# Weight blocks 160 instead of 128 columns apart in the panels that multiply x, and a separate buffer for the norms' sums

## What is computed

```
for l in range(2):
    hn = rmsnorm(x, g_mix_pre[l])
    m  = mixer_even(hn) if l == 0 else mixer_odd(hn)     # hn @ w_in (1024 x 2048, or 1024 x 3072),
                                                         # gating or recurrence or short convolution,
                                                         # then @ w_out (1024 x 1024)
    x  = x + rmsnorm(m, g_mix_post[l])
    hn = rmsnorm(x, g_ffn_pre[l])
    f  = square(relu(hn @ mlp_up[l])) @ mlp_down[l]      # 1024 x 4096 and 4096 x 1024
    x  = x + rmsnorm(f, g_ffn_post[l])
```

## Time and profile before

| | |
|---|---|
| median of 3 runs | 2115.69 us |
| the profiled execution | 2116.21 us |
| its span in the trace | 2114.1 us |
| TensorE busy (matmuls) | 2105.2 us, 100% of the span |
| VectorE (DVE) busy | 1187.2 us, 56% |
| ScalarE (ACT) busy | 718.6 us, 34% |
| GpSimd (POOL) busy | 279.3 us, 13% |
| mean granted TensorE clock | 0.999 of full speed |

### The profile page before, as it was taken

How to read it: one execution, slowest core, us unless ns; L and a number is a source line. 1 busy time by engine, 2 the same in 40 slices (tenths; PEclk the granted TensorE clock), 3 DMA queues, 4 the chain that set the end, 5 groups by cost and what they waited for, 6 DMA issues and landing times.

```text
span 2114.1 us, 33629 instructions
## 1 busy us (share of the span) xinstructions
PE 2105.2 (100%) x13976; PEld 2094.1 (99%) x13976; DVE 1187.2 (56%) x1798; ACT 718.6 (34%) x1225; POOL 279.3 (13%) x307
## 2 busy tenths in 40 slices
PE   9999999999999999999999999999999999999998
PEld 9999999999999999999999999999999999999998
DVE  8766367364755747334953333384566475564336
ACT  6673345132232322333511112352313233232332
POOL 2000000031221312000033232000113022130000
PEclk9999999999999999999999999999999999999999
DMA  4111422111111111141311114131111111111142
GB/s 165 39 38 40 137 78 85 51 51 42 51 48 51 51 51 51 42 141 40 123 51 40 51 50 133 41 122 51 45 52 45 51 51 51 51 51 46 46 142 82
DMA packets 209189, 138.78 MB, mean 66 GB/s; under 512 B 6768, under 2 KB 205552, under 8 KB 209040
## 3 DMA queue, kind: packets, MB, share of 16 engines
q1 hardware_dynamic: 208320, 135.51, 21.1%
q10 hardware_dynamic: 720, 1.13, 0.1%
HBM read 119.22 MB, written 17.40 MB: 65 GB/s over the span
## 4 chain that ended last, share of the span: by engine, by line
PE 89%; issue 10%; DMA 0%; POOL 0%; DVE 0%; DVEq 0%; ACTq 0%; SPq 0%; POOLq 0%
PE ps L881 23%; PE ps L882 23%; PE ps L883 23%; PE ps L927 6%; PE ps L929 6%; PE ps L930 6%; PE ps L1003 1%; PE ps L1031 0%; PE ps L957 0%; PE ps L948 0%; DMA w_all_raw<-in_w_in_even_dram 0%; PE ps L944 0%; DMA w_all_raw<-in_mlp_down_dram 0%; PE ps L1014 0%; PE ps L990 0%
## 5 line engine op out<-in xcount | busy, mean ns | idle before, releaser
L881 PE MATMUL ps<-x_hi,w_all 128*128 128x352 f32 x2304 | 751.4, 326 | 0.0
L883 PE MATMUL ps<-x_hi,w_all 128*128 128x352 f32 x2304 | 739.4, 321 | 0.0
L882 PE MATMUL ps<-x_lo,w_all 128*128 128x352 f32 x2304 | 739.3, 321 | 0.0
L882 PEld LDWEIGHTS ps<-x_lo,w_all 128*128 128x128 f32 x2304 | 433.6, 188 | 2.2
L881 PEld LDWEIGHTS ps<-x_hi,w_all 128*128 128x128 f32 x2304 | 432.6, 188 | 2.7
L883 PEld LDWEIGHTS ps<-x_hi,w_all 128*128 128x128 f32 x2304 | 432.3, 188 | 0.0
L1116 ACT CAST w_all<-w_all_raw 128x1024 fp32r<-128x1024 f32 (+1 forms) x166 | 199.8, 1204 | 422.0 <-DMA w_all_raw<-in_mlp_up_dram 167.6
L927 PE MATMUL ps<-h_hi,w_all 128*128 128x264 f32 x1120 | 318.9, 285 | 0.0
L929 PE MATMUL ps<-h_lo,w_all 128*128 128x264 f32 x1120 | 318.6, 284 | 0.0
L930 PE MATMUL ps<-h_hi,w_all 128*128 128x264 f32 x1120 | 318.0, 284 | 0.0
L1635 DVE SCALAR_TENSOR_TENSOR tmp<-ps,rstd 128x352 f32<-128x352 f32 x192 | 100.1, 522 | 284.6 <-PE ps L883 284.5
(11 more groups left out here) (225 smaller groups left out, 2415.5 us busy)
## 6 DMA issues: line engine op xcount, KB each, us to landing
w_all_raw<-in_mlp_up_dram SPq DMA_DIRECT2D x60, 512.0 KB, 3.9
w_all_raw<-in_mlp_down_dram SPq DMA_DIRECT2D x96, 256.0 KB, 3.1
x_save<-f SPq DMA_DIRECT2D x9, 1408.0 KB, 6.5
x_old<-x_save SPq DMA_DIRECT2D x9, 1408.0 KB, 11.7
w_all_raw<-in_c_w_in_dram SPq DMA_DIRECT2D x22, 512.0 KB, 3.6
w_all_raw<-in_w_in_even_dram SPq DMA_DIRECT2D x12, 512.0 KB, 3.6
w_all_raw<-in_mlp_down_dram SPq DMA_DIRECT2D x12, 512.0 KB, 4.0
x_old<-in_x_cols_dram SPq DMA_DIRECT2D x3, 1408.0 KB, 11.2
```

What stands on the lines that cost most here:

```text
L881: nc.tensor.matmul(dst, wh, hi, start=(i == 0), stop=False)
L882: nc.tensor.matmul(dst, wh, lo, start=False, stop=False)
L883: last = nc.tensor.matmul(dst, wl, hi, start=False, stop=(i == len(order) - 1))
```

## The change

The change touches two places. In the panels of `w_in_even`, `c_w_in` and `mlp_up` that lie in a rotating slot, the blocks of 128 columns lie 160 columns apart: the high part takes 1280 columns, and the low part and the raw data begin at column 1280 instead of 1024. Two such parts (2560 columns) now reach over the place where `sq_sum` and `fold` lay, so these get a buffer `sums` of their own behind the others.

```diff
-        sq_sum = [w_all_raw[:, 0, 2 * D + t * TT:2 * D + (t + 1) * TT].rearrange("p (j c) -> p j c", c=QUAD)
-                  for t in range(NT)]
-        fold = [w_all_raw[:, 0, 2 * D + NT * TT + 16 * i:2 * D + NT * TT + 16 * i + NJ] for i in range(8)]
+        sums = place("sums", [P, TOK + 8 * 16], F32)
+        sq_sum = [sums[:, t * TT:(t + 1) * TT].rearrange("p (j c) -> p j c", c=QUAD) for t in range(NT)]
+        fold = [sums[:, TOK + 16 * i:TOK + 16 * i + NJ] for i in range(8)]
         root, rcol = fold[6], fold[7]
...
             if slot in ROTATING:
                 s = ROTATING.index(slot)
-                size = FORMS if LOADS[l].pair else D
-                three = [w[:, s, i * size:(i + 1) * size].rearrange("p (k n) -> p k n", n=P)
+                step = P + 32 if LOADS[l].name[0] in ("w_in_even", "c_w_in", "mlp_up") else P
+                size = FORMS if LOADS[l].pair else KC * step
+                three = [w[:, s, i * size:(i + 1) * size].rearrange("p (k n) -> p k n", n=step)[:, :, 0:P]
                          for w, i in ((w_all, 0), (w_all, 1), (w_all_raw, 1))]
```

## The result

| | before | after |
|---|---|---|
| median | 2115.77 us (8 runs, 2115.56 to 2116.10) | 2121.66 us (8 runs, 2121.43 to 2122.09) |
| profiled execution | 2116.21 us | 2121.43 us |
| its span | 2114.1 us | 2119.4 us |

The changed kernel takes 1.0028 of the time before (95% interval 1.0019 to 1.0036), 5.9 us more. 2121.7 was forecast.

What follows compares the result with a forecast made beforehand. The prediction took TensorE, by the distance of matmul starts, to bound the kernel. To the median of 2115.69 it added 6.0 us (5.8 on TensorE, 0.2 by DMA), giving 2121.7 us, range 2115.5 to 2126.5.

Steps and rivals of the forecast that it cites:

- What bounds it: TensorE, busy 2105.2 of 2114.1 us: the time is the number of matmuls by the distance of their starts.
- The parity rule: Moving and weight blocks in the same 128-byte half of a 256-byte period (even distance) are dearer: strip 1, 0.05 us.
- The size on TensorE: x units with weights in `w_all`: 0.00, 0.05 and 0.01 us more in strips 0, 1 and 2, 5.8 us in all.
- in `w_all` ... all strips take the same: Units with weights in `w_all` before the change: odd and even alternate by block, so strips took 3.82, 3.81, 3.82 us.
- The DMA's short runs: `w_in_even` loads cut into 512-byte runs: 0.2 us at the start, later panels' slots free a panel (11.45 us) ahead.
- all covers gone: Upper end at the start: without cover behind the first load, each further half load costs as much, 0.8 us.
- a quiet row: Profile row for quiet times: 512 KB lands in 3.6 us from `w_in_even`, 3.9 from `mlp_up`; short runs cost at most 0.4.
- The sums' buffer, ACT and DVE: ACT's copy and DVE's subtraction over gaps, and norms' sums at a new address: each 0 us.
- The sum: Whole kernel: 5.8 us on TensorE and 0.2 by DMA, 6.0 more on a median of 2115.69, giving 2121.7 us.
- the second rival: TensorE's x units: steady odd strips 0 and 2 gain 11.5 us, strip 1 loses 7.0; 2111.2 us, chance 0.09.
- the third: Third rival, TensorE's x units: all strips slow, as the third product meets the other half; 14.4 us, 2130.3, chance 0.05.
- The two read ports: Skill's rule for TensorE: two independent SBUF read ports, so weight loads take no bandwidth from the running matmul; term 0.

Runs made afterwards that it cites:

- experiment 2: Against the changed kernel, weight blocks of the x panels 192 columns apart instead of 160, so the parity alternates again: 2117.72 us (1.0009).
- experiment 3: Against the changed kernel, each x panel begins 32 columns (128 bytes) later in its slot: 2126.28 us (1.0049).
- experiment 7: Against the changed kernel, blocks 224 columns apart in `c_w_in` and `mlp_up`, 128 in `w_in_even`: 2119.27 us (1.0016).
- experiment 11: Against the kernel before, strips of `x_hi` and `x_lo` 384 columns apart instead of 352, so every x distance is even: 2121.37 us (1.0026).
- experiment 12: Against the kernel before, strips 384 columns apart and each x panel 128 bytes later, so every x distance is odd: 2113.45 us (0.9988).
- experiment 8: Against the changed kernel, only the low part of each x panel begins 128 bytes later: 2125.70 us (1.0047).
- experiment 9: Against the changed kernel, blocks back at 128 columns and the low part of each x panel 128 bytes later: 2118.16 us (1.0011).
- experiment 4: Against the changed kernel, the first four panels keep blocks 128 columns apart: 2120.50 us (1.0022).
- experiment 5: Against the changed kernel, blocks 192 columns apart in `c_w_in` and `mlp_up`, 128 in `w_in_even`: 2115.85 us (1.000).
- experiment 6: Against the changed kernel, blocks 160 columns apart in `c_w_in` and `mlp_up` alone, 128 in `w_in_even`: 2119.29 us (1.0016).
- experiment 1: Against the changed kernel, blocks back at 128 columns, sums still in their own buffer: 2115.89 us (1.000).
- experiment 10: Against the changed kernel, blocks back at 128 columns and each x panel 64 bytes later in its slot: 2121.64 us (1.0027).

## Why the prediction was right, and where it wasn't

- **What bounds it.** Right in the main: all but 1.4 us of the growth lies in TensorE's own distances, and h units and Strassen groups kept their time to 0.1 us in all. The 1.4 are the DMA's, see below.
- **The parity rule.** Right where it was used: a panel in the changed kernel takes strip for strip what the panel in `x_hi` took. Shown by experiments 2, 3 and 7: neither gap, strip nor longer period counts, a shift of 128 bytes turns the strips over; and by the panels in `x_hi` of experiments 11 and 12. As a rule for other layouts it fell short. It said that an even distance is dear, by 0.05 us a unit; then units in which odd and even alternate should have stood halfway, near 3.84, but they took 3.81 to 3.82 in its own rows. Experiments 11 and 12 fit these: all even 3.84, all odd 3.80, and 3.82 is their mean. The 3.87 is the price of another pattern, even in the first two products and odd in the third, and experiments 8 and 9 show too that the order of the parities over the products counts. The forecast held because the panel in `x_hi` had the same pattern in all three.
- **The size on TensorE.** 5.8 us forecast, 3.8 measured (-0.8, +4.3, +0.3). The step that failed is "in `w_all` ... all strips take the same", which I read from one panel. Not all units of before were at 3.82. The `mlp_up` panel behind a Strassen group started its strips, before, at:

```profile
492.48 0.33 PE L881 MATMUL ps<-x_hi,w_all 128*128 128x352 f32 x1
...
496.36 0.32 PE L881 MATMUL ps<-x_hi,w_all 128*128 128x352 f32 x1
...
500.21 0.32 PE L881 MATMUL ps<-x_hi,w_all 128*128 128x352 f32 x1
...
504.02 0.32 PE L881 MATMUL ps<-x_hi,w_all 128*128 128x352 f32 x1
```

  3.88, 3.85, 3.81. After the change the same panel starts at 494.44, 498.27, 502.14, 505.96: 3.83, 3.87, 3.82. In the ten such panels strip 0 gained 0.05 us, and strip 1 lost 0.02 instead of 0.05. In the panels that share a stretch with `ha` and `hb`, strip 0 gained 0.05 and strip 2 gained 0.06. Strip 2 lost 0.01 in most panels, as forecast, but not as strip 2: in the twenty panels whose strips run backwards it lost nothing, and strip 0, which there stands behind the slow strip 1, lost the 0.01 (3.818 to 3.827 in the mean). So the 0.01 goes with the place behind a slow unit.
- **The DMA's short runs.** 0.2 us forecast (at most 0.8 with all covers gone), about 1.4 measured in the profiled pair: 0.7 at the start and 0.7 at the gates. For the start I scaled a quiet row (3.9 against 3.6) and looked at the first load alone, which landed as before (6.17); a load behind it landed 0.9 us later and took over the chain, and the first plain unit came 0.9 us later in the mean of fourteen kernels. The quiet row was no clean measure either: the loads of `c_w_in`, cut into runs of 512 bytes in both kernels, took 3.6 in both. For the later panels I wrote that they land a panel ahead; that was said from the slots, without a look at ACT's waits for them (7.7 us in four waits in the stretch 23 to 210 before, 9.7 after). Experiments 2, 4, 5 and 6 show both: with long runs in `w_in_even` the gates' waits are gone, with short ones and unslowed units they are there.
- **The sums' buffer, ACT and DVE.** Nothing, as forecast (experiment 1; the copy takes 1.05 us in both).
- **The sum.** +3.8 on TensorE and +1.4 by the DMA make 5.2, against 5.8 + 0.2 = 6.0: two errors of 2.0 and 1.2 us that largely cancel. The 0.8 that is left is hidden by how the two profiled executions fell, 5.2 apart where the medians are 5.9 apart. The time was right to 0.1 us by luck.
- **A slip.** What the shortest and longest records could give is in the second rival, not in the third as the prediction says.
- **The two read ports.** The rule of the Trainium skill ("TensorE: Matmul & The Clock Gate", section "Step-by-step: what each phase is for") gave 0 for TensorE's term. The traces don't agree: by it experiments 10, 11 and 12, with the same long runs, should take the same time, and so should experiment 3 and the changed kernel, with the same short ones. The first three lie between 2113.45 and 2121.64 us, the other two at 2126.28 and 2121.66.

What stays open: what in the hardware has a period of 256 bytes, and which pair of reads meets. Experiment 8 shows that it isn't simply the moving block and the weight block loaded beside it, product by product. No run tried h panels in `w_all`, or the pairs, with other distances. A version that keeps the layout all odd and stays out of the 4.00 us gait wasn't tried either, and what starts or ends that gait isn't known.

## What to carry to other kernels

In this kernel TensorE is fed without a gap and each matmul has fresh weights, and still the distance between two starts depends on the addresses of both operands: in one and the same panel, a unit of 24 equal matmuls took from 3.80 to 3.92 us by where its blocks lie within 256 bytes. In a kernel like it, look for the same work with its operands elsewhere in the trace and compare the distances of starts, strip by strip, in several places, also behind an interruption. And when an edit cuts a contiguous load into pieces, look at every queue that already waits for that load, not at the slot that it fills.

## What the runs showed of the hardware that I had not expected

- The two gaits: with all distances odd a unit takes 3.80 us in most places and 4.00 us in stretches of several units (16 whole units: four in the first layer between 42 and 74 us, the others beside `ha` and `hb`), without a wait and at a granted clock of 0.999 over the kernel. So the addresses of a unit alone don't tell its time; what came before it counts. The same shows before the change, in the 3.88 us of the unit behind a Strassen group.
- With all distances even no unit takes 4.00 us: 3.84 us in each strip, panel behind a Strassen group included (493.47, 497.31, 501.14, 504.99). But it has a second pace as well: the last six units of `w_in_even` (197.87 to 221.07) take 3.87 us each, where with all distances odd they take 3.80.
- A shift of 64 bytes for the x panels cost 5.8 us in a kernel of 2116 with nothing else changed but the place of the sums, which costs nothing (experiments 10 and 1).
